# First-layer expert rows for 32 dense tokens from gathered rows, and VectorE's second-layer work in pairs of tiles

## The chip, the cores and the metric

The kernel runs on one NeuronCore of a Trainium2 chip. A core has TensorE (matmuls; its weight loads are listed as PEld beside PE), VectorE (DVE), ScalarE (ACT), GpSimd (POOL), the issuing queue SyncE (SP) and 16 DMA engines that all queues share. The metric is device time in microseconds (us) from launch to end, the median of several runs; lower is better.

## What is computed

The program is two transformer blocks on one sequence of 512 tokens of width 1024. The part that matters here is the last one, a PEER layer: 16,384 experts, each of them one row `u` and one row `v` of 1024 numbers. Each token picks 16 experts for each of 8 heads, so 128 picks:

```
q = (xb @ w_pq).reshape(PEER_BLOCK, PEER_HEADS, 2, D_KEY // 2)
s = einsum("thpd,hpnd->thpn", q, sub_keys)
s_top, i_top = lax.top_k(s, PEER_TOPK)
cand = s_top[:, :, 0, :, None] + s_top[:, :, 1, None, :]
best, ci = lax.top_k(cand, PEER_TOPK)
e = i1 * N_KEYS + i2
gate = softmax(best)
act = gelu(einsum("thkd,td->thk", u_exp[e], xb))
out = einsum("thk,thkd->td", gate * act, v_exp[e])
```

## The kernel before, in words

The PEER layer is done in two ways. For the first 128 tokens (one per partition) the picked rows are **gathered**: GpSimd issues an indirect DMA that brings 128 rows of 4 KB (one per token), VectorE multiplies the `u` rows with the tokens and sums them (`dot`, L1965, a custom instruction), and later adds the `v` rows times their coefficients to a sum in PSUM (`axpy`, L2097). 128 picks make 128 dots and 128 row sums. Seven row buffers (`GR`) rotate: a gather waits until the row seven places before it has been used.

For the other `TD` = 384 tokens the layer is **dense**, over all 16,384 experts in `NE` = 128 tiles of 128 experts. In the **first layer** (`up(e)`, L2795) TensorE multiplies a `u` tile with the 384 tokens: 8 chunks of the width times 3 products, since every 32-bit operand is split in a high and a low half (high times high, high times low, low times high). ScalarE makes the high half of a weight tile (`split_high`, L1368), GpSimd the low half (`split_low`, L867), into one of two buffers; `split_high(e + 2)` waits until `up(e)` has finished. ScalarE applies gelu (L1374) and SP stores the activations to DRAM (`expert_acts`). Meanwhile VectorE searches the picks (`for t in range(NT)`), and from tile `FIRST_SPREAD` = 52 on, for 48 tiles, the gates are spread: per tile VectorE builds one-hot matrices for 8 tokens (L2081, L2082, L2084), TensorE multiplies them (16 short matmuls, L2812), and ScalarE stores the product, a gate for each token and expert (0 where not picked), to `gates_spread` in DRAM.

In the **second layer** (`down(e, c)`, L2825) SP loads activations and gates back, VectorE multiplies them (`weigh`, L2107), ScalarE and VectorE split the product (`weighted_high`, L1402; `weighted_low`, L2113), and TensorE multiplies it with the `v` tile: 2 halves of the width times 3 groups of 128 tokens times 3 products, 18 matmuls of 512 columns per tile. The low half of even `v` tiles comes from GpSimd (L867), that of odd ones from VectorE (`odd_low`, L2120), in four buffers (`WS`).

The order on each engine is written out by hand. GpSimd issues gather j behind the `split_low` of the tile that `gather_after(j)` names. VectorE runs dots inside the search (`between`), after each one-hot batch (5 for 3 batches), and in the second layer `axpys_by(e)` row sums, 14 for 13 tiles, from tile 4 on.

## Time and profile before

| | |
|---|---|
| three runs | 2490.09, 2494.13, 2505.22 us, median 2494.13 |
| profiled execution, span | 2489.0 us |
| PE busy | 2441.9 us (98%) |
| DVE busy | 1589.9 us (64%) |
| POOL busy | 1304.9 us (52%) |
| ACT busy | 961.0 us (39%) |
| DMA | 508.91 MB, mean 204 GB/s |
| granted TensorE clock, mean | 0.997 of full speed |

The profiled execution's own time is not listed apart from these three; its span is 1.1 us below the fastest of them and 5.1 us below the median. Times in rows are microseconds from the start of the span, "mean ns" is one instruction. The time in brackets at the end of a row is how long the engine sat idle before it, and what ended that. The first layer of the experts runs from about 1321 to 1944 us, the second from 1944 to about 2471.

### The profile page before, as it was taken

What the parts mean: (1) busy time and instruction counts of PE and PEld (TensorE: products, weight loads), DVE (VectorE), ACT (ScalarE), POOL (GpSimd) and SP (SyncE); (2) the same over time, 40 slices, a digit from 0 to 9 for tenths busy, and PEclk for the clock granted to TensorE, in tenths of its full rate; (3) what the DMA queues carried; (4) which work ended last, traced back from release to release, by engine and by line L of the source; (5) the groups of instructions that cost most, each with busy time, mean ns of one, the idle gap of its engine ahead of it and who ended that gap; (6) DMA issues with size and microseconds to landing.
All of it is one profiled execution on the core that took longest, in us unless ns stands there. A gap on an engine that the chain in (4) does not pass through costs nothing.

```text
span 2489.0 us, 32824 instructions
## 1 busy us (share of the span) xinstructions
PE 2441.9 (98%) x12339; PEld 2069.7 (83%) x12339; DVE 1589.9 (64%) x2580; ACT 961.0 (39%) x1565; POOL 1304.9 (52%) x698
## 2 busy tenths in 40 slices
PE   9999999999999999999999999999999999999998
PEld 6877766778786777787789999999999888888886
DVE  3247255766403635332479897998940799999995
ACT  3256455222224445523333334343433433333333
POOL 3651423444454433144434887666666566676662
PEclk9999999999999999999999999999999999999999
DMA  5320112655433222032223888999997899999992
GB/s 215 119 85 1 60 60 95 199 196 177 153 102 118 85 78 76 26 102 91 95 85 125 297 304 283 359 354 361 359 320 258 304 363 360 364 368 362 363 364 88
DMA packets 212733, 508.91 MB, mean 204 GB/s; under 512 B 18400, under 2 KB 101344, under 8 KB 212192
## 3 DMA queue, kind: packets, MB, share of 16 engines
q1 hardware_dynamic: 123696, 338.22, 38.8%
q0 software_dynamic: 36864, 134.23, 15.1%
q10 hardware_dynamic: 52016, 34.36, 4.4%
q8 instruction: 99, 1.62, 0.3%
q14 instruction: 58, 0.48, 0.1%
HBM read 454.31 MB, written 52.43 MB: 204 GB/s over the span
## 4 chain that ended last, share of the span: by engine, by line
PE 89%; POOL 3%; DVE 3%; ACT 3%; issue 1%; DMA 1%; SPq 0%; ACTq 0%; DVEq 0%
PE bank L2211 73%; PE bank L2812 3%; PE bank_and L2211 3%; POOL weight_split L851 3%; PE bank L2346 3%; PE bank_and L2179 2%; PE bank L2336 1%; ACT weight_split L992 1%; DMA ring<-weights 1%; PE bank_and L2311 1%; PE bank L2311 1%; PE bank L2190 0%; PE bank_and L2625 0%; DVE h_split L1471 0%; POOL weight_split L867 0%
## 5 line engine op out<-in xcount | busy, mean ns | idle before, releaser
L2211 PE MATMUL bank<-h_split,weight_split 128*128 128x384 f32 (+1 forms) x5568 | 1135.3, 362 | 16.1 <-POOL weight_split L851 6.6
L2211 PEld LDWEIGHTS bank<-h_split,weight_split 128*128 128x128 f32 x5568 | 995.1, 188 | 130.5 <-POOL weight_split L851 16.4
L851 POOL TENSOR_TENSOR weight_split<-ring,weight_split 128x1024 fp32r<-128x1024 f32 x182 | 453.8, 2494 | 721.3 <-ACT weight_split L992 721.1
L2211 PE MATMUL bank<-late_weight_split,weighted_split 128*128 128x512 f32 x2268 | 515.1, 389 | 0.2 <-DVE weighted_split L2113 0.2
L2211 PEld LDWEIGHTS bank<-late_weight_split,weighted_split 128*128 128x128 f32 x2268 | 425.4, 188 | 88.9 <-issue 0.6
L878 POOL DMA_INDIRECT arena<-weights,arena x256 | 312.6, 1221 | 147.0 <-DVE arena L1965 60.0
L867 POOL TENSOR_TENSOR weight_split<-ring,weight_split 128x1024 fp32r<-128x1024 f32 x129 | 310.1, 2404 | 120.5 <-ACT weight_split L1368 119.5
L992 ACT ACTIVATE weight_split<-ring 128x1024 fp32r<-128x1024 f32 x182 | 191.9, 1054 | 293.4 <-PE bank L2211 273.8
L1368 ACT ACTIVATE weight_split<-ring 128x1024 fp32r<-128x1024 f32 x130 | 137.6, 1060 | 390.6 <-PE bank L2211 335.3
L2107 DVE TENSOR_TENSOR arena<-arena 128x384 f32<-128x384 f32 x128 | 227.0, 1773 | 20.3 <-DMA arena<-expert_acts 19.9
L867 POOL TENSOR_TENSOR late_weight_split<-ring,late_weight_split 128x1024 fp32r<-128x1024 f32 x63 | 151.9, 2411 | 103.7 <-ACT late_weight_split L1368 103.1
L1965 DVE CUSTOM_DVE_ANT_0 arena<-arena,bank_and 128x1024 f32<-128x1024 f32 x128 | 153.1, 1218 | 47.8 <-DMA arena<-weights,arena 46.8
L1402 ACT ACTIVATE weighted_split<-arena 128x384 fp32r<-128x384 f32 x128 | 67.3, 526 | 269.4 <-DVE arena L2107 258.8
L2097 DVE SCALAR_TENSOR_TENSOR bank_and<-arena,bank_and 128x1024 f32<-128x1024 f32 x127 | 162.6, 1281 | 0.9
L1368 ACT ACTIVATE late_weight_split<-ring 128x1024 fp32r<-128x1024 f32 x126 | 132.6, 1052 | 46.6 <-PE bank L2211 40.9
L2211 PE MATMUL bank<-hidden_layer_split,weight_split 128*128 128x512 f32 x528 | 122.3, 392 | 1.3 <-POOL weight_split L851 1.0
L2211 PEld LDWEIGHTS bank<-hidden_layer_split,weight_split 128*128 128x128 f32 x528 | 98.2, 188 | 25.0 <-issue 2.6
L1533 DVE SCALAR_TENSOR_TENSOR arena<-bank,rstd 128x512 f32<-128x512 f32 x42 | 29.0, 692 | 124.4 <-PE bank L2211 116.1
L2113 DVE TENSOR_TENSOR weighted_split<-arena,weighted_split 128x384 fp32r<-128x384 f32 x128 | 74.1, 579 | 47.3 <-ACT weighted_split L1402 47.3
L2812 PE MATMUL bank<-arena 128*128 128x128 f32 x768 | 93.4, 275 | 0.0
L2812 PEld LDWEIGHTS bank<-arena 128*128 128x128 f32 x768 | 92.3, 192 | 0.0
L2346 PEld LDWEIGHTS bank<-arena 128*128 128x128 f32 x528 | 67.4, 191 | 22.0 <-ACT arena L1027 13.4
(367 smaller groups left out, 2724.7 us busy)
## 6 DMA issues: line engine op xcount, KB each, us to landing
ring<-weights SPq DMA_DIRECT2D x493, 512.0 KB
expert_acts<-arena SPq DMA_DIRECT2D x128, 192.0 KB
gates_spread<-arena ACTq DMA_DIRECT2D x24, 1024.0 KB
arena<-gates_spread SPq DMA_DIRECT2D x96, 256.0 KB
arena<-expert_acts SPq DMA_DIRECT2D x128, 192.0 KB
arena<-weights,arena POOLq DMA_INDIRECT x256
arena<-bias_sel ACTq DMA_DIRECT2D x1, 2048.0 KB, 7.7
arena<-bias_band ACTq DMA_DIRECT2D x1, 2048.0 KB, 8.2
```

The lines of the kernel that those rows point to most:

```text
L851: nc.gpsimd.tensor_tensor(w_split[:, (count - 1) % 2, 1, :], ring[:, n % RING, :], w_split[:, (count - 1) % 2, 0, :], ALU.subtract).then_i ...
L867: nc.gpsimd.tensor_tensor(w[:, 1, :], ring[:, (BEFORE + e) % RING, :], w[:, 0, :], ALU.subtract).then_inc(w_lo_ready, 1)
L878: nc.gpsimd.indirect_dma_start(gathered_rows[:, j % GR, :], None, expert_rows, bass.IndirectOffsetOnAxis(ap=pick, axis=0)).then_inc(gather ...
L992: a.activation(w_split[:, s % 2, 0, :], ring[:, n % RING, :], ACT.Copy).then_inc(w_high, 1)
L1368: a.activation(split_of(e)[:, 0, :], ring[:, n % RING, :], ACT.Copy).then_inc(w_hi_ready, 1)
L1965: v.tensor_tensor_reduce(rows_, rows_, wide[:, :], 1.0, 0.0, ALU.mult, ALU.add, dots[:, j:j + 1]).then_inc(gather_used, 1)
L2097: v.scalar_tensor_tensor(out=wide[:, :], in0=rows_, scalar=coef[:, j:j + 1], in1=wide[:, :], op0=ALU.mult, op1=ALU.add).then_inc(gather_us ...
L2107: v.tensor_tensor(weighed[:, e % 2, :], act_in[:, e % AS, :], gblk[:, b % 2, :, j], ALU.mult).then_inc(weighed_ready, 1)
L2113: v.tensor_tensor(p_split[:, e % PS, 1, :], weighed[:, e % 2, :], p_split[:, e % PS, 0, :], ALU.subtract).then_inc(p_lo_ready, 1)
L2211: ins = mm(*args, start=start, stop=stop)
L2346: last = mm(bank[4 + g % 2][:, h * HD:(h + 1) * HD], probT[:, u % 2, c * P:(c + 1) * P], vals(i, c), start=(c == 0), stop=(c == blocks(i) ...
L2812: mm(bank[2 + n % 3][:, (t % 4) * P:(t % 4 + 1) * P], hot1[:, t % HOT, :], hot2[:, t % HOT, :], start=True, stop=True).then_inc(hot_used, 1)
```

## The change

Of the 384 dense tokens the first `XC` = 32 leave the dense first layer, so `up(e)` works on `TU` = 352 tokens and the stored activations are 352 wide. The 32 tokens have 32 x 128 = 4096 picks; laid out as 128 partitions by `CC` = 32 columns (four partitions for a token) they are 32 more gathers and dots, ahead of the 128 of the first kind. Their tokens are repeated four times by ScalarE (`few_wide`) and put into PSUM by 16 matmuls; row numbers go out to DRAM and back in the new layout, and so do the finished dots, after which ScalarE applies gelu and VectorE multiplies them into the gates before the gates are spread. In the second layer the activations of these 32 tokens are a constant 1.0 (one memset), so their products with the spread gates are already complete. The second layer of the 32 tokens stays dense.

The search takes the tokens in the order 1, 0, 2, 3; `FIRST_SPREAD` goes from 52 to 56; 3 dots for 2 batches run in place of 5 for 3. Of 160 dots 128 are done by the end of the first layer, the other 32 in the second, tiles 2 to 24; the 128 row sums follow from tile 26 to 120. Both come at 8 for 3 pairs of tiles. VectorE's second-layer loop is written per pair.

```diff
+XC = 32
+CC = PICKS * XC // P
+TU = TD - XC
+UP_ROWS = CC + PICKS
...
-        FIRST_SPREAD = 52
-        SPREAD_DOTS = TOP_DOTS + BATCHES * 5 // 3
-        AXPY_FROM = 4
+        FIRST_SPREAD = 56
+        SPREAD_DOTS = TOP_DOTS + BATCHES * 3 // 2
+        UP_DOTS = SPREAD_DOTS + 20
+        AXPY_FROM = 26
...
+        def dots_by(e):
+
+            return min(UP_DOTS + e // 2 * 8 // 3, UP_ROWS)
...
-            return min(max((e - AXPY_FROM + 1) * 14 // 13, 0), PICKS)
+            return min(max((e - AXPY_FROM) // 2 + 1, 0) * 8 // 3, PICKS)
...
             if j < GR:
-                return 13 + j * 2 // 3
+                return 15 + j * 2 // 3
             n = j - GR
             if n < TOP_DOTS:
-                return 17 + n
+                return 18 + n
...
+                if e == FEW_ROWS_AT:
+                    sp.wait_ge(rows_ready, 1)
+                    sp.dma_start(by_token[0], few_rows).then_inc(few_moved, 16)
+                elif e == FEW_ROWS_AT + 1:
+                    sp.wait_ge(few_moved, 16)
+                    sp.dma_start(few_row_at, turned_dram[0]).then_inc(few_moved, 16)
+                elif e == FEW_DOTS_AT:
+                    sp.wait_ge(gather_used, CC)
+                    sp.dma_start(turned_dram[1], few_dots).then_inc(few_moved, 16)
+                elif e == FEW_DOTS_AT + 1:
+                    sp.wait_ge(few_moved, 48)
+                    sp.dma_start(few_gelu, by_token[1]).then_inc(few_moved, 16)
...
-            for t in range(NT):
+            for t in SEARCH_ORDER:
...
+                if t == 1:
+                    dve.wait_ge(dots_gelu, 1)
+                    v.tensor_tensor(gates_[0:XC], gates_[0:XC], few_gelu, ALU.mult).then_inc(chosen_ready, 1)
...
-                dots_to(TOP_DOTS + (batch + 1) * 5 // 3)
-            dots_to(PICKS)
+                dots_to(TOP_DOTS + (batch + 1) * 3 // 2)
+            link(v.memset(act_in[:, :, 0:XC], 1.0))
+            dots_to(UP_DOTS)
...
             weigh(0)
+            weigh(1)
+            weighted_low(0)
+            odd_low(NE + 1)
+            weighted_low(1)
             summed = 0
-            for e in range(NE):
-                if e + 1 < NE:
-                    weigh(e + 1)
-                    if e == 0:
-                        weighted_low(e)
-                    if (e + 1) % 2:
-                        odd_low(NE + e + 1)
-                if e:
-                    weighted_low(e)
-                if e == AXPY_FROM - 1:
-                    dve.wait_ge(dots_gelu, 1)
+            for e in range(2, NE, 2):
+                dve.wait_ge(w_hi_ready, NE + e + 1)
+                if e == AXPY_FROM:
+                    dve.wait_ge(dots_gelu, 2)
                     link(v.tensor_tensor(coef, dots, gate0, ALU.mult))
+                dots_to(dots_by(e))
                 while summed < axpys_by(e):
                     axpy(summed)
                     summed += 1
+                weigh(e)
+                weigh(e + 1)
+                weighted_low(e)
+                weighted_low(e + 1)
+                odd_low(NE + e + 1)
...
-                    x = [h_split[:, part, k, P:T] for part in range(2)]
-                    last = products(bank[e % 2][:, 0:TD], w, x, k == 0, k == KD - 1)
+                    x = [h_split[:, part, k, P + XC:T] for part in range(2)]
+                    last = products(bank[e % 2][:, 0:TU], w, x, k == 0, k == KD - 1)
```

How the order moves on VectorE, in the middle of the second layer. L2097 before and L2158 now is the row sum, L2107 and L2168 `weigh`, L2120 and L2181 `odd_low`, L2113 and L2174 `weighted_low`; `weighted_split_61` holds the split product, `late_weight_split_62` the split weights. Before:

```order
L2097 SCALAR_TENSOR_TENSOR bank6_and_7<-arena,bank6_and_7 128x1024 [waits gathered_rows_used,rows_gathered4]
L2107 TENSOR_TENSOR arena<-arena 128x384 [waits p_lo_ready,act_loaded1]
L2120 TENSOR_TENSOR late_weight_split_62<-ring,late_weight_split_62 128x1024 [waits w_hi_ready]
L2113 TENSOR_TENSOR weighted_split_61<-arena,weighted_split_61 128x384 [waits p_hi_ready]
L2097 SCALAR_TENSOR_TENSOR bank6_and_7<-arena,bank6_and_7 128x1024 [waits gathered_rows_used,rows_gathered5]
L2107 TENSOR_TENSOR arena<-arena 128x384 [waits p_lo_ready,act_loaded2]
L2113 TENSOR_TENSOR weighted_split_61<-arena,weighted_split_61 128x384 [waits p_hi_ready]
```

and now:

```order
L2158 SCALAR_TENSOR_TENSOR bank6_and_7<-arena,bank6_and_7 128x1024 [waits gathered_rows_used,rows_gathered0,w_hi_ready]
L2158 SCALAR_TENSOR_TENSOR bank6_and_7<-arena,bank6_and_7 128x1024 [waits gathered_rows_used,rows_gathered1]
L2168 TENSOR_TENSOR arena<-arena 128x384 [waits p_lo_ready,act_loaded0,gates_loaded0]
L2168 TENSOR_TENSOR arena<-arena 128x384 [waits p_lo_ready,act_loaded1]
L2174 TENSOR_TENSOR weighted_split_61<-arena,weighted_split_61 128x384 [waits p_hi_ready] x2
L2181 TENSOR_TENSOR late_weight_split_62<-ring,late_weight_split_62 128x1024 [waits w_hi_ready]
```

The row sums (here two, in two pairs of three it is three) stand together at the head of a pair, behind a wait for the high half of the pair's even weight tile; the two `weigh`, the two `weighted_low` and the `odd_low` follow them.

On GpSimd, in the same stretch, `DMA` rows are gathers and `TENSOR_TENSOR` rows the low half of even tiles. Before:

```order
L878 DMA arena<-weights,arena 128x1024 [waits gathered_rows_used] x2
L867 TENSOR_TENSOR late_weight_split<-ring,late_weight_split 128x1024 [waits w_hi_ready]
L878 DMA arena<-weights,arena 128x1024 [waits gathered_rows_used] x3
L867 TENSOR_TENSOR late_weight_split<-ring,late_weight_split 128x1024 [waits w_hi_ready]
L878 DMA arena<-weights,arena 128x1024 [waits gathered_rows_used] x2
```

and now:

```order
L907 TENSOR_TENSOR late_weight_split<-ring,late_weight_split 128x1024 [waits w_hi_ready]
L921 DMA arena<-weights,arena 128x1024 [waits gathered_rows_used] x3
L907 TENSOR_TENSOR late_weight_split<-ring,late_weight_split 128x1024 [waits w_hi_ready]
L921 DMA arena<-weights,arena 128x1024 [waits gathered_rows_used] x2
L907 TENSOR_TENSOR late_weight_split<-ring,late_weight_split 128x1024 [waits w_hi_ready]
```

Behind each low half come two or three gathers, three in two cases of three; before it was two, and three once in every six or seven.

## Rows read from the trace of the kernel before

**Rows 1.** Windows: length, busy (instructions) per engine, clock, DMA share, GB/s.

```profile
1950.00:2430.00 480.00, 479.18 (x2113) 396.43 (x2114) 476.25 (x421) 180.37 (x237) 324.27 (x181) 1.00 0.99 363
1560.00:1824.00 264.00, 264.00 (x1777) 264.00 (x1776) 241.31 (x286) 107.38 (x179) 178.97 (x120) 1.00 1.03 358
```

**Rows 2.** Timeline of PE, last first-layer tiles: start, length, line, tiles, count.

```profile
1827.87 116.73 PE L2211 MATMUL bank<-h_split,weight_split 128*128 128x384 f32 x672
```

**Rows 3.** Timeline of PE, late in the second layer.

```profile
2399.79 63.64 PE L2211 MATMUL bank<-late_weight_split,weighted_split 128*128 128x512 f32 x280
```

**Rows 4.** Timeline, ScalarE and GpSimd in a plain first-layer tile.

```profile
1940.54 1.06 ACT L1368 ACTIVATE weight_split<-ring 128x1024 fp32r<-128x1024 f32 x1 [2.72 <-PE bank L2211]
...
1941.68 2.40 POOL L867 TENSOR_TENSOR weight_split<-ring,weight_split 128x1024 fp32r<-128x1024 f32 x1 [1.77 <-ACT weight_split L1368]
```

**Rows 5.** Timeline of three engines where PE did wait for GpSimd.

```profile
1547.42 4.12 PEld L2211 LDWEIGHTS bank<-h_split,weight_split 128*128 128x128 f32 x24
...
1551.82 2.37 POOL L867 TENSOR_TENSOR weight_split<-ring,weight_split 128x1024 fp32r<-128x1024 f32 x1
1551.95 1.06 ACT L1368 ACTIVATE weight_split<-ring 128x1024 fp32r<-128x1024 f32 x1 [3.54 <-PE bank L2211]
...
1554.30 1.86 PEld L2211 LDWEIGHTS bank<-h_split,weight_split 128*128 128x128 f32 x11 [0.86 <-ACT arena L1374]
```

**Rows 6.** Timeline of GpSimd at the first gathers.

```profile
1372.85 2.40 POOL L867 TENSOR_TENSOR weight_split<-ring,weight_split 128x1024 fp32r<-128x1024 f32 x1 [1.74 <-ACT weight_split L1368]
1375.41 1.15 POOL L878 DMA_INDIRECT arena<-weights,arena  x1 [0.17 <-issue]
...
1377.83 2.41 POOL L867 TENSOR_TENSOR weight_split<-ring,weight_split 128x1024 fp32r<-128x1024 f32 x1
```

**Rows 7.** Timeline, steady second layer: GpSimd, VectorE and ScalarE.

```profile
2197.42 2.40 POOL L867 TENSOR_TENSOR late_weight_split<-ring,late_weight_split 128x1024 fp32r<-128x1024 f32 x1
2197.62 2.95 DVE L2107 TENSOR_TENSOR arena<-arena 128x384 f32<-128x384 f32 x1
...
2201.03 1.04 ACT L1368 ACTIVATE late_weight_split<-ring 128x1024 fp32r<-128x1024 f32 x1
2202.15 0.88 DVE L2107 TENSOR_TENSOR arena<-arena 128x384 f32<-128x384 f32 x1
2202.50 1.35 POOL L878 DMA_INDIRECT arena<-weights,arena  x1 [1.10 <-DVE bank_and L2097]
2202.94 1.22 DVE L2120 TENSOR_TENSOR late_weight_split<-ring,late_weight_split 128x1024 fp32r<-128x1024 f32 x1
2203.06 0.53 ACT L1402 ACTIVATE weighted_split<-arena 128x384 fp32r<-128x384 f32 x1 [0.99 <-DVE arena L2107]
2204.08 0.55 DVE L2113 TENSOR_TENSOR weighted_split<-arena,weighted_split 128x384 fp32r<-128x384 f32 x1
```

**Rows 8.** Timeline of VectorE, two row sums back to back.

```profile
2433.03 2.67 DVE L2097 SCALAR_TENSOR_TENSOR bank_and<-arena,bank_and 128x1024 f32<-128x1024 f32 x2
```

**Rows 9.** The page, costliest groups: the dots on VectorE.

```profile
L1965 DVE CUSTOM_DVE_ANT_0 arena<-arena,bank_and 128x1024 f32<-128x1024 f32 x128 | 153.1, 1218 | 47.8 <-DMA arena<-weights,arena 46.8
```

**Rows 10.** The page, DMA issues: count and KB each.

```profile
ring<-weights SPq DMA_DIRECT2D x493, 512.0 KB
expert_acts<-arena SPq DMA_DIRECT2D x128, 192.0 KB
...
arena<-gates_spread SPq DMA_DIRECT2D x96, 256.0 KB
```

**Rows 11.** Windows of 8.16 us in the second layer.

```profile
2023.44:2031.60 8.16, 8.16 (x38) 6.76 (x37) 8.16 (x9) 3.06 (x4) 5.21 (x4) 1.00 1.03 402
2096.88:2105.04 8.16, 8.16 (x38) 6.76 (x37) 8.16 (x9) 3.06 (x4) 5.20 (x4) 1.00 0.92 284
```

**Rows 12.** Timeline at the change of layers: PE and VectorE.

```profile
1950.63 4.35 PE L2211 MATMUL bank<-weight_split,weighted_split 128*128 128x512 f32 x18 [1.91 <-DVE weighted_split L2113]
...
1952.07 0.90 DVE L2107 TENSOR_TENSOR arena<-arena 128x384 f32<-128x384 f32 x1 [1.58 <-DMA arena<-expert_acts]
```

More of the change, by code:

```diff
@@ L884, in _ @@
                     split_low(e)
-                while issued < 2 * PICKS and gather_after(issued) <= e:
+                while issued < UP_ROWS + PICKS and gather_after(issued) <= e:
                     gather(issued)
                     issued += 1
-            assert issued == 2 * PICKS
+            assert issued == UP_ROWS + PICKS
             for k in range(1, 4):
@@ L1975, in between @@
             def between(t):
-                if t and dotted[0] < TOP_DOTS // ND * t:
+                if dotted[0] < TOP_DOTS // ND * SEARCH_ORDER.index(t):
                     dots_to(dotted[0] + 1)
@@ L2816, in _ @@
                 up(e)
+                if e == 2:
+                    pe.wait_ge(few_spread, 2)
+                    pe.wait_ge(score_out, 16)
+                    for k in range(KD):
+                        for part in range(2):
+                            last = mm(few_x[:, k * P:(k + 1) * P], few_wide[:, part, k, :], ident, start=(part == 0),
+                                      stop=(part == 1))
+                    last.then_inc(x_rows, 1)
                 if e == FIRST_SPREAD - 1:
```

87 lines of the change are left out of this document (61 added, 26 removed).

## Prediction, made before the changed kernel was run

> **What bounds the kernel now.** I read the windows first. In the second layer [rows 1] PE is busy 479 of 480 us, VectorE 476, and the DMA share is 0.99 at 363 GB/s: three resources stand at their limit together. In the first layer with its one-hot batches PE is busy 264 of 264 us and DMA has a share of 1.03. The granted clock is 1.00 of 2.4 GHz in both. So PE sets the time of the whole stretch that the change touches, and the question is which of the others takes over where PE is relieved or they are loaded. The timelines give PE's pace: 672 matmuls of 384 columns in 116.73 us, 173.5 ns each [rows 2], 24 to a tile, so 4.163 us a tile; 280 of 512 columns in 63.64 us, 226.7 ns each [rows 3], 18 to a tile, 8.16 us for a pair. With a one-hot batch there are 40 matmuls per tile, 1777 in 264 us [rows 1], 5.94 us a tile; a batch of 16 costs 1.78.
>
> **First layer, the matmuls.** The two widths give the price of a column: (226.7 - 173.5) / 128 = 0.416 ns. Cutting 32 columns saves 13.3 ns each, 0.32 us a tile: 3.84 in place of 4.163. In the 48 tiles with a batch PE has only itself to wait for: 48 x 0.32 = 15.3 us.
>
> The other 80 tiles cannot take all of it. Split weights have two buffers, so tile e + 2 is bound to the end of tile e: from the first weight load of a tile to ScalarE's next high half 4.53 us (1547.42 to 1551.95) [rows 5], from there to GpSimd's start 1.14 and GpSimd 2.40 [rows 4], and 0.11 until PE loads (GpSimd ends at 1554.19, PE starts at 1554.30) [rows 5]. That is 8.18 for two tiles, against 8.33 that PE needs: now hidden by 0.15. With 352 columns the loop is 8.18 - 0.32 = 7.86, 3.93 a tile, and PE would need only 3.84. So the loop decides: 80 x (4.163 - 3.93) = 18.6 us. What was cover becomes the bound, and GpSimd's lateness costs directly from here on.
>
> **First layer, what is added.** 16 matmuls of 128 columns after tile 2: a batch, 1.8 us. Spreading the tokens is two ScalarE instructions of 1024 columns, 1.06 each by the high half [rows 4], in a tile with over 2 us of idle ScalarE: nothing. SP gets four small transfers with waits; the ring is four tiles ahead, so its cover is over 10 us, and it would cost only if the 32 dots were not done by tile 47: nothing. GpSimd's first gathers come two to a tile, and there its halves start 4.98 us apart [rows 6], 0.8 above PE's present need and 1.05 above 3.93. The change has such tiles at 15 and 17 and one of three gathers at 19. I count 3.2 us against 1.2 now: 2.0. The exponentials are issued two whole tiles ahead of the turn of the gates, a lead that shrinks by 2 x 0.23: 0.5 us if it had none to spare, and I charge that.
>
> **The change of layers.** PE waits 1.91 us for VectorE's low half of tile 1, which the new order makes earlier: gone. Late next is tile 2: its low half now stands behind the multiply of tile 3, whose activations land at 1952.07 [rows 12]; 0.90 and 0.55 more make 1953.5, where PE is due 4.08 after 1948.72, at 1952.8. 0.7 remains, 1.2 us are saved.
>
> Together 15.3 + 18.6 - 1.8 - 2.0 - 0.5 + 1.2 = 30.8 us saved before the second layer's pace is asked.
>
> **Second layer.** PE's work is unchanged, 8.16 a pair. Two things could become longer. First **VectorE**. Now one multiply of each pair starts beside GpSimd's subtraction and takes 2.95 us in place of 0.88, ending 0.75 after it [rows 7]. The row sums, which read PSUM, and the dots, 1218 ns on average [rows 9], show no such lengthening. The new order puts them beside the subtraction: two sums take 2.67 [rows 8], the subtraction 2.40 [rows 7], and both start on the same signal. The chain of a pair is then: 8/3 sums at 1.33, 3.55; multiply 0.88; ScalarE's copy, high half and copy, 0.53 + 1.04 + 0.53; VectorE's low half 0.55 and odd split 1.22 [rows 7, 8]. That is 8.27 with every end fully awaited; instructions that follow on one engine start some 0.09 before the last one ends (2202.15 + 0.88 against 2202.94) [rows 7], four times, so 7.9. PE has 8.16: no cost at 7.9, 7 us in 60 pairs at 8.27. I take 0. GpSimd has 2.40 and 8/3 gathers at 1.35 [rows 7], 6.0.
>
> Second **DMA**. A pair moved two weight tiles, two activation tiles, one and a half gate blocks [rows 10] and 28/13 gathers of 512 KB: 2.96 MB in 8.16 us, 363 GB/s, just what the window shows, so DMA moved what was asked. Now the activations fall to 176 KB and the gathers rise to 8/3: 3.20 MB, 392 GB/s. The ends: windows in the second layer reach 402 GB/s [rows 11], which would cost nothing; 363 as a ceiling would make a pair 8.82, 60 x 0.66 = 40 us more. The window with 284 GB/s at a share of 0.92 [rows 11] shows that the rate also falls without an idle queue. I take the upper end, less a little for such dips: 3 us. The nearest row is the one of 402, since it is the same mix at a demand above average.
>
> A rule speaks against that choice. The Trainium skill, "DMA: Bandwidth & Descriptors", section "Where 436 GB/s comes from", puts the limit of one core's HBM traffic at about 358 GB/s and the vendor's model at 368. At 358 a pair would take 8.94 us and the stretch 47 us more, an estimate by which the kernel would be some 16 us slower than before. The trace already holds 363 over 480 us and 402 for a while, so the first figure is not a ceiling here; the measurement decides, though nothing shows 392 for long.
>
> **Sum.** 30.8 - 3 = 28 us. Against the profiled span of 2489.0 that is 2461; the median of the runs lies 5.1 above the span, so 2466.
>
> **The rivals.**
> DMA becomes the bound in the second layer. For it: share 0.99 already, the dips, 19% more gathered bytes per pair. Against: 402. A ceiling of 380 makes a pair 8.42 and costs 16 us, a kernel of 2479; 363 gives 2503.
> The loop over two buffers is not there, PE keeps its 13.3 ns everywhere and GpSimd's lateness is absorbed: 128 x 0.32 = 40.8, less 1.8 and 0.5, plus 1.2, 39.7 saved: 2454. Against it stands the sum of rows 4 and 5.
> The chain of VectorE and ScalarE is 8.27 or a little more: 2473 to 2480.
> The matmuls do not get shorter, since the weight loads bind: PEld is busy 264.00 of 264 us in the first layer [rows 1], and the number of loads stays. Then 33.9 is lost and the kernel takes about 2500. The Trainium skill, "Perfetto Trace Analysis", section "Identifying the Most-Contended Engine", tells to judge TensorE by the busy share of LDWEIGHTS, and by that PE has no headroom here. Against it: 16 short matmuls take 1.78 us [rows 1, 2], 111 ns for a load and a product, so loads can follow each other far faster than every 173 ns.
> Slower: the multiplies still meet the subtraction. GpSimd's subtraction stands in line behind gathers, each of which waits for the row sum seven places before; if the last gather of a pair ends late, the subtraction starts late and holds both the multiply and the chain behind it, 2.95 - 0.88 = 2.07 us a pair. In all 60 pairs: 7.9 + 2.07 = 9.97 against 8.16, 109 us, a kernel of 2572. Below 0.26 us a pair it costs nothing, and it makes the kernel slower than before once it takes 0.77 a pair, some four pairs in ten. Against it: GpSimd has 2 us to spare in a pair, and its gathers can all be issued by about 7 us.
>
> **Chances.** Forecast 0.48 (2457 to 2474), DMA 0.23, no loop 0.08, the longer chain 0.08, loads bind 0.04, multiplies still held 0.09. The range takes the forecast, the fast rival, and DMA down to about 365 GB/s: 2452 to 2500. One per cent, 25 us, is about what can be told from no change here. Faster by more: the forecast below 2469, 0.40, and the fast rival, 0.08: 0.48. Slower by more: held multiplies and a worse DMA, 0.11. Between: 0.41.
>
> **What would show it.** In the profile after: first-layer matmuls 160 ns apart in tiles with a batch and tiles of 3.93 without, with short waits of PE for GpSimd's half in the latter; if the tiles are 3.84, the loop was wrong; if 4.16, the columns. In the second layer PE pairs of 8.16, multiplies of 0.88 and none of 2.95, DMA near 390 GB/s. PE waiting there for VectorE's low half, while VectorE waits for activations or gathered rows, means that DMA bounds. What would make the forecast wrong first is the rate that DMA can hold, then any regular lateness of GpSimd.

## The result and the profile after

The changed kernel takes **2466.9 us** (median of 17 runs, 2463.33 to 2494.76), the kernel before 2491.63 (17 runs, 2489.45 to 2505.22). The ratio is 0.9903, 95% interval 0.9885 to 0.9921: 24.7 us less. The forecast was 2466 in a range of 2452 to 2500. That the number agrees does not make the terms right. The profiled execution has a span of 2469.1 us (2470.95 with what lies around it); against the profiled 2489.0 of before it saves 19.9 where the prediction's sum said 28.

The same windows as in [rows 1], a little shorter in the second layer because the kernel ends earlier:

```profile
1950.00:2400.00 450.00, 449.75 (x1985) 372.19 (x1984) 397.35 (x452) 161.35 (x224) 335.56 (x202) 1.00 1.03 399
1560.00:1824.00 264.00, 262.57 (x1818) 262.41 (x1818) 239.67 (x280) 108.79 (x184) 175.43 (x116) 1.00 1.03 348
```

PE is still full in both. VectorE, to which work was added, shows less busy time (88% against 99%), and DMA moves 399 GB/s where it moved 363. PE in the first layer (start, length, line, tiles, count, wait ahead), which answers to [rows 2]:

```profile
1331.20 3.73 PE L2886 MATMUL bank_and<-const,arena 128*128 128x128 f32 x32
...
1386.93 7.84 PE L2275 MATMUL bank<-h_split,weight_split 128*128 128x352 f32 x48 [0.55 <-POOL weight_split L907]
1395.23 7.85 PE L2275 MATMUL bank<-h_split,weight_split 128*128 128x352 f32 x48 [0.46 <-POOL weight_split L907]
1404.78 142.19 PE L2275 MATMUL bank<-h_split,weight_split 128*128 128x352 f32 x864 [1.69 <-POOL weight_split L907]
...
1554.93 4.05 PE L2275 MATMUL bank<-h_split,weight_split 128*128 128x352 f32 x24
...
1562.19 4.05 PE L2275 MATMUL bank<-h_split,weight_split 128*128 128x352 f32 x24 [1.43 <-POOL weight_split L907]
...
1567.78 4.24 PE L2275 MATMUL bank<-h_split,weight_split 128*128 128x352 f32 x24
1571.85 1.95 PE L2876 MATMUL bank_and<-arena 128*128 128x128 f32 x16
1573.56 4.24 PE L2275 MATMUL bank<-h_split,weight_split 128*128 128x352 f32 x24
```

There are two tile lengths beside the one-hot batches: 4.05 to 4.07 for the first three tiles and 4.24 for the other 45, at a granted clock of 1.00. The first matmul of such a row takes 0.24 to the second and the last 0.33; the 22 steps between are 158 ns in the short row and 167 in the long one. A tile with its batch takes 5.78 (1567.78 to 1573.56); it was 5.94, and 5.62 was forecast. In the plain tiles 864 matmuls, 36 tiles, run in 142.19 us: 3.950 a tile, forecast 3.93. The starts of the single matmuls show that this is a mean of two things: 25 of the 35 tiles between the first start and the last one have the pitch of 158 ns and take 3.92, with a stall of 0.1 to 0.2 us at the end of nearly every second one, and 10 have 166 to 167 ns and take 4.02. The matmuls of `few_x` are 32 in the profile and take 3.5 us.

The first layer begins at 1319.46 (before 1321.21, in code that was not touched), its batches at 1549.32 and the second layer at 1924.15. With the same places of before, against the sum on record:

| part, profiled spans | before | after | saved | forecast |
|---|---|---|---|---|
| up to the first layer | 1321.21 | 1319.46 | 1.75 | 0 |
| 80 plain tiles with `few_x` and waits | 334.55 | 323.81 | 10.7 | 18.6 - 1.8 - 2.0 = 14.8 |
| turn of the gates | 2.26 | 2.32 | -0.1 | -0.5 |
| 48 tiles with a batch | 286.42 | 278.56 | 7.9 | 15.3 |
| second layer to the end | 544.56 | 544.95 | -0.4 | 1.2 - 3 = -1.8 |
| sum | 2489.0 | 2469.1 | 19.9 | 27.8 |

PE's waits for others around the first layer (total us, times, longest), which hold what [rows 5] and [rows 12] were about:

```profile
PE bank L2275 <- POOL weight_split L907: 6.0, 6, 1.7
PE bank_and L2275 <- DVE weighted_split L2174: 2.3, 3, 1.4
PE bank L2275 <- DVE arena L2130: 1.1, 1, 1.1
```

VectorE's multiplies `weigh` and GpSimd's low halves in 1960 to 2400, before and after (count, busy us, mean ns of one, idle time before them):

```profile
L2107 DVE TENSOR_TENSOR arena<-arena 128x384 f32<-128x384 f32 x109 | 197.0, 1807 | 0.0
```

```profile
L2168 DVE TENSOR_TENSOR arena<-arena 128x384 f32<-128x384 f32 x108 | 92.9, 900 | 3.9 <-DMA arena<-expert_acts 3.9
```

```profile
L907 POOL TENSOR_TENSOR late_weight_split<-ring,late_weight_split 128x1024 fp32r<-128x1024 f32 x55 | 153.2, 2786 | 74.7 <-ACT late_weight_split L1411 74.7
```

So the multiplies of 2.95 us of [rows 7] are gone, as forecast; GpSimd's low half, 2.40 in [rows 7], is now 2.79 on average. It now starts while `odd_low` is still running, and is longer by about the time that the two overlap:

```profile
2161.51 1.22 DVE L2181 TENSOR_TENSOR late_weight_split<-ring,late_weight_split 128x1024 fp32r<-128x1024 f32 x1
2162.03 2.96 POOL L907 TENSOR_TENSOR late_weight_split<-ring,late_weight_split 128x1024 fp32r<-128x1024 f32 x1 [1.32 <-ACT late_weight_split L1411]
```

Of the 55 low halves in 1960 to 2400, those that overlap `odd_low` by 0.7 us take 2.94 to 2.97, and the ten that overlap it by 0.1 or less take 2.40 or 2.41; `odd_low` itself stays at 1.22. The row sums beside them make no difference to either.

### The profile page after: what moved, and what is told of

Read it like the earlier page. It is cut to its first block, busy times and chain, and to the rows that moved or that the text cites. A ratio compares the mean times of both kernels' runs of the same rounds, so it can differ in the third digit from the quotient of the medians.

```text
span 2469.1 us, 33014 instructions
## 1 busy us (share of the span) xinstructions
PE 2420.5 (98%) x12371; PEld 2040.6 (83%) x12371; DVE 1532.1 (62%) x2649; ACT 951.0 (39%) x1568; POOL 1332.3 (54%) x730
## 4 chain that ended last, share of the span: by engine, by line
PE 87%; POOL 4%; DVE 3%; ACT 3%; DMA 2%; issue 1%; SPq 0%; ACTq 0%; DVEq 0%
PE bank L2275 60%; PE bank_and L2275 14%; PE bank L2410 3%; POOL weight_split L891 2%; PE bank_and L2876 2%; PE bank_and L2243 2%; PE bank_and L2400 1%; PE bank L2876 1%; DMA ring<-weights 1%; ACT weight_split L1035 1%; POOL weight_split L907 1%; DMA arena<-expert_acts 1%; PE bank_and L2375 1%; PE bank L2375 1%; PE bank L2748 0%
## 5 line engine op out<-in xcount | busy, mean ns | idle before, releaser
L2275 PE MATMUL bank<-h_split,weight_split 128*128 128x352 f32 (+1 forms) x5472 | 1086.1, 356 | 17.2 <-POOL weight_split L907 6.0
L2275 PEld LDWEIGHTS bank<-h_split,weight_split 128*128 128x128 f32 x5472 | 943.9, 188 | 133.6 <-issue 15.2
L2275 PE MATMUL bank<-late_weight_split,weighted_split 128*128 128x512 f32 x1512 | 363.8, 390 | 0.0
L2275 PEld LDWEIGHTS bank<-late_weight_split,weighted_split 128*128 128x128 f32 x1512 | 283.7, 188 | 58.8
L907 POOL TENSOR_TENSOR late_weight_split<-ring,late_weight_split 128x1024 fp32r<-128x1024 f32 x63 | 175.7, 2789 | 106.4 <-ACT late_weight_split L1411 106.4
L2018 DVE CUSTOM_DVE_ANT_0 arena<-arena,bank_and 128x1024 f32<-128x1024 f32 x160 | 191.2, 1217 | 62.4 <-DMA arena<-weights,arena 60.9
L2275 PE MATMUL bank_and<-late_weight_split,weighted_split 128*128 128x512 f32 x756 | 192.2, 390 | 2.3 <-DVE weighted_split L2174 2.3
L2158 DVE SCALAR_TENSOR_TENSOR bank_and<-arena,bank_and 128x1024 f32<-128x1024 f32 x127 | 163.4, 1286 | 12.1 <-ACT late_weight_split L1411 3.4
L2275 PEld LDWEIGHTS bank_and<-late_weight_split,weighted_split 128*128 128x128 f32 x756 | 141.7, 188 | 32.8 <-issue 3.5
L2168 DVE TENSOR_TENSOR arena<-arena 128x384 f32<-128x384 f32 x128 | 117.9, 960 | 13.2 <-DMA arena<-expert_acts 10.4
L2174 DVE TENSOR_TENSOR weighted_split<-arena,weighted_split 128x384 fp32r<-128x384 f32 x128 | 72.8, 569 | 66.0 <-ACT weighted_split L1445 65.0
L2275 PE MATMUL bank_and<-h_split,weight_split 128*128 128x512 f32 x384 | 91.8, 396 | 0.3 <-POOL weight_split L891 0.3
```

Of the source, the lines that this page charges most:

```text
L907: nc.gpsimd.tensor_tensor(w[:, 1, :], ring[:, (BEFORE + e) % RING, :], w[:, 0, :], ALU.subtract).then_inc(w_lo_ready, 1)
L2018: v.tensor_tensor_reduce(rows_, rows_, x[:, :], 1.0, 0.0, ALU.mult, ALU.add, n).then_inc(gather_used, 1)
L2158: v.scalar_tensor_tensor(out=wide[:, :], in0=rows_, scalar=coef[:, j:j + 1], in1=wide[:, :], op0=ALU.mult, op1=ALU.add).then_inc(gather_us ...
L2168: v.tensor_tensor(weighed[:, e % 2, :], act_in[:, e % AS, :], gblk[:, b % 2, :, j], ALU.mult).then_inc(weighed_ready, 1)
L2174: v.tensor_tensor(p_split[:, e % PS, 1, :], weighed[:, e % 2, :], p_split[:, e % PS, 0, :], ALU.subtract).then_inc(p_lo_ready, 1)
L2275: ins = mm(*args, start=start, stop=stop)
```

## The experiments

Four questions were open: whether the added work costs anything beside the narrower matmul; what the pairs are worth; why a tile with a batch takes 5.78 and not 5.62; and how near the second layer stands to DMA's limit. Twelve runs follow, two of them of the changed kernel itself. Each is compared with the kernel before on its own chip; where only parts are compared, the places are the same as in the table above.

### The changed kernel again

> The changed kernel once more, beside the other kernels of this group on one chip. Expected: 2467 us, within 2.

2473.3 us, median of 4 runs (2465.05 to 2475.93), ratio 0.9899 (0.9851 to 0.9946). Run again with the last three kernels:

> The changed kernel once more, as the one that the next three are held against on the same chip. Expected: 2467 to 2473 us, the values that it had before.

2465.3 us, 6 runs (2463.92 to 2474.6), ratio 0.9883 (0.9857 to 0.9909). The profiled spans were 2473.3 and 2472.8. PE's waits for GpSimd differed, 5.4 and 7.0 us in 8, and the first layer began at 1319.64 and 1321.43. The first lies outside the 2 us that were expected. So the kernel scatters by some 10 us, and single profiles must be compared part by part.

### The narrower matmul alone

```diff
 # the kernel before
+XC = 32
-    x = [h_split[:, part, k, P:T] for part in range(2)]
-    last = products(bank[e % 2][:, 0:TD], w, x, ...)
+    x = [h_split[:, part, k, P + XC:T] for part in range(2)]
+    last = products(bank[e % 2][:, 0:TD - XC], w, x, ...)
```

> The kernel before, with its first expert layer on 352 columns in place of 384 and nothing else; the first layer of 32 tokens of the dense block is left out and a constant stands in its place (no gathered rows, no added dots, no few_x matmuls, no pairs). Theory: the whole gain is the narrower matmul, and what the change adds beside it costs 1.8 (few_x) and about 2 (waits for the first gathers) on TensorE. Then this kernel is at 2467 less 4, 2463. Within it, a plain tile is 3.95 us or a little less, and a tile beside a gate batch goes from 5.94 to 5.78 if the 166.7 ns pitch of 352 columns belongs to the width and to a fully fed TensorE, to 5.56 if that pitch came from something that the change added (the dots, the gathers). Rival: the 166.7 ns pitch is the added work's doing; then 48 x 0.22 = 10.6 more is saved, and the time is 2452.

2468.7 us, 10 runs (2458.4 to 2485.53), ratio 0.9896 (0.9867 to 0.9925). Its profile gives 320.66 us for the plain tiles, 276.38 for the batches and 545.04 for the rest, from the start of the first layer 1144.3 in place of 1149.6: 5.3 us below the changed kernel. The time is 4.6 us below the changed kernel run beside it, and the ranges overlap. So the narrower matmul brings all the gain, and the added work costs a few us (4 was expected): 3.2 in the plain tiles. The 2.2 in the batches are in part the pitch, as follows. Of the 48 tiles beside a batch, 26 took 4.24 or 4.26 and 22 took 4.04 or 4.05, without dots or gathers of the change:

```profile
1690.76 4.24 PE L2214 MATMUL bank<-h_split,weight_split 128*128 128x352 f32 x24
1694.84 1.05 PE L2815 MATMUL bank<-arena 128*128 128x128 f32 x8
1696.51 1.16 PE L2815 MATMUL bank<-arena 128*128 128x128 f32 x8 [0.62 <-ACT arena L1385]
1697.43 4.05 PE L2214 MATMUL bank<-h_split,weight_split 128*128 128x352 f32 x24
1701.32 1.95 PE L2815 MATMUL bank<-arena 128*128 128x128 f32 x16
```

The slow pitch belongs to this width, and here it ended behind a wait of 0.62 us. A wait does not always end it: in the first run of the changed kernel again a tile behind a wait of 1.42 is slow,

```profile
1564.47 4.24 PE L2275 MATMUL bank<-h_split,weight_split 128*128 128x352 f32 x24 [1.42 <-POOL weight_split L907]
```

where the same tile behind 1.43 took 4.05 above. The theory's 5.78 a tile is there, and beside it 5.59 (1552.23 to 1557.82), near the rival's 5.56.

### Pairs alone, and the change without pairs

```diff
 # the kernel before; only VectorE's order
-            for e in range(NE):
-                if e + 1 < NE:
-                    weigh(e + 1)
...
+            for e in range(2, NE, 2):
+                dve.wait_ge(w_hi_ready, NE + e + 1)
...
+                weigh(e)
+                weigh(e + 1)
+                weighted_low(e)
+                weighted_low(e + 1)
+                odd_low(NE + e + 1)
```

> The kernel before with VectorE's second-layer work in pairs of tiles, and nothing else: all 384 dense columns stay on TensorE. Theory: TensorE sets the second layer at 4.08 us a tile with and without pairs, so 2491 us, within 2; the multiplies of the weights by the gates fall from 1.77 us to about 0.96 us each, because in a pair they stand clear of GpSimd's subtraction, and VectorE's busy time falls by about 100 us, none of it on the path. Rival: VectorE was late at some tiles of the second layer and pairs alone take 5 to 10 us off: 2482 to 2486. Third: work in pairs hands the first tile of a pair over later, and TensorE waits: above 2495.

2489.4 us, 10 runs (2487.71 to 2504.66), ratio 0.9975 (0.995 to 1.0): no change that can be told, as the theory had it. The multiplies fell to 0.91 us (0.96 was expected) and VectorE's busy time in 1950 to 2400 by 80 us, from 446 to 366 (100 was expected). The reverse experiment takes the changed kernel and undoes the pairs:

```diff
 # the changed kernel; only VectorE's order and its rates
-            for e in range(2, NE, 2):
+            for e in range(NE):
+                if e + 1 < NE:
+                    weigh(e + 1)
...
-    return min(UP_DOTS + e // 2 * 8 // 3, UP_ROWS)
+    return min(UP_DOTS + max(e - 1, 0) * 4 // 3, UP_ROWS)
```

> The changed kernel with VectorE's second-layer work back in single tiles, the dots and row sums of the gathered rows spread at the same mean rate (4/3 a tile). Theory: the pairs are what makes room for the added dots. The multiplies go back from 0.96 to 1.77 us each, 128 x 0.81 = 104 us, which on top of VectorE's 397 of 450 us makes 501: a tile takes at least 4.5 us in place of 4.08 and the kernel about 2467 + 51 = 2518, range 2500 to 2530. Rival: the longer multiplies hold time in which VectorE has nothing to do (they wait for GpSimd's subtraction and something else waits less), and the time stays within 5 of 2467.

2469.5 us, 4 runs (2462.1 to 2476.88), ratio 0.9887 (0.9835 to 0.9938). The theory said 2518 and is wrong; the rival holds. Its windows and multiplies in the second layer:

```profile
1950.00:2400.00 450.00, 450.00 (x1987) 372.63 (x1986) 446.37 (x454) 166.96 (x223) 351.19 (x205) 1.00 1.02 395
```

```profile
L2168 DVE TENSOR_TENSOR arena<-arena 128x384 f32<-128x384 f32 x109 | 157.1, 1442 | 0.0
```

The kernel before in the same window:

```profile
1950.00:2400.00 450.00, 449.18 (x1980) 371.60 (x1981) 446.25 (x395) 169.01 (x222) 307.16 (x172) 1.00 0.99 364
```

VectorE does 454 instructions in the same 446 us of busy time in which it did 395. That is 32 more rows used, since a dot has two records, the second of 0.08 us. The room came from the multiplies themselves: 1807 ns on average before, 1442 here, 900 in pairs; 109 multiplies became 40 us shorter in all, and 32 rows at 1.22 to 1.28 us are 40 us. In the 1807 there is a time in which the multiply stands held beside GpSimd's subtraction [rows 7], and it is booked as busy. **Busy time of that kind is slack.** VectorE's 99% was not a bound.

### The pitch of a matmul and its width

The kernel before on 368 and on 320 columns, one run each, edited like the one on 352 (`XC = 16`, `XC = 64`).

> The kernel before with its first expert layer on 368 columns (the first layer of 16 tokens is left out). It asks what a matmul's pitch is as its width goes. At 384 columns it was 173.3 ns in every tile, at 512 226.7 ns, both 32 cycles over the width. Theory: two pitches, one of 32 cycles over the width when weight loads fit, one of 400 cycles (166.7 ns) that is the width's or the weight load's floor in a fully fed TensorE. Then 368 columns take 400 cycles in every tile, batch or plain: 24 x 166.7 ns = 4.00 us, and a tile beside a gate batch takes the same 5.78 us as with 352 columns. Rival: the pitch is a fixed surplus of 28 or 48 cycles, then 165.0 or 173.3 ns.

> The kernel before with its first expert layer on 320 columns (the first layer of 64 tokens is left out). Theory: beside the gate batches a fully fed TensorE has a floor of 400 cycles (166.7 ns) a matmul, set by its weight loads; 320 columns then gain nothing over 352 there: 5.78 us a tile. In plain tiles the loop over the split buffers holds 3.9 us or a little less. Rival: the pitch goes on falling with the width, to 352 or 368 cycles (146.7 or 153.3 ns), and the batch tiles take 5.3 to 5.46 us; then the kernel is about 48 x 0.4 = 19 us faster than with 352 columns, as far as the GpSimd loop lets it.

Tiles beside a batch, of 368 columns, a row of plain ones of 368, and tiles of 320 beside a batch and in the plain part:

```profile
1691.67 4.24 PE L2214 MATMUL bank<-h_split,weight_split 128*128 128x368 f32 x24
...
1398.82 52.36 PE L2214 MATMUL bank<-h_split,weight_split 128*128 128x368 f32 x312
```

```profile
1692.83 3.76 PE L2214 MATMUL bank<-h_split,weight_split 128*128 128x320 f32 x24
...
1406.46 7.39 PE L2214 MATMUL bank<-h_split,weight_split 128*128 128x320 f32 x48 [0.17 <-POOL weight_split L869]
1414.01 7.39 PE L2214 MATMUL bank<-h_split,weight_split 128*128 128x320 f32 x48 [0.16 <-POOL weight_split L869]
```

At 368 columns a tile takes 4.24 beside a batch and 4.03 in the plain part (52.36 us for 13), 167 ns apart in both: the same as the slow pitch of 352. The expectation for 368 held, the one of a floor did not: at 320 columns all 48 tiles beside batches took 3.75 to 3.79 us, 147 ns apart, as its rival said. With 384 columns at 173.5 and 512 at 226.7 [rows 2, 3], four widths lie on one line of (columns + 32) / 2.4 ns. Only 352 is off it, at 158 or 167 and never the 160 of the line. So **beside the batches 352 columns cost what 368 cost** (batches 278.6 us in the changed kernel and 279.2 here), and the second half of the columns that the change removes pays only in the plain tiles. The times were 2473.3 and 2440.6 us, one run each, beside 2489.4 for before.

The 320 rows show the loop over the two split buffers as well: it takes 7.55 us for two plain tiles (1406.46 to 1414.01), with a wait for GpSimd in each of these rounds. The prediction's loop of 8.18 less 64 columns is 7.54, where PE alone would need 7.04. Where the profile lists no wait, as in a row of 336 matmuls in 52.86 us, two tiles still take 7.55: the stalls are below what it lists.

### A small matmul ahead of each tile

```diff
                 pe.wait_ge(w_lo_ready, e + 1)
+                if FIRST_SPREAD < e <= FIRST_SPREAD + BATCHES:
+                    mm(bank[e % 2][:, 0:8], w_split[:, e % 2, 0, 0:P], h_split[:, 0, 0, P + XC:P + XC + 8], start=True, stop=True)
                 for k in range(KD):
```

> The changed kernel with one matmul of 8 columns ahead of each first-layer tile that follows a one-hot batch (its result is overwritten). In the changed kernel a 352-column matmul took 166.7 ns in those tiles and 158.3 ns after TensorE had waited. Theory: the two pitches are two phases between the weight loads and the matmuls, which a wait resets and a short matmul may reset too. If it does, a tile beside a batch saves 24 x 8.3 ns = 0.20 us and pays 0.07 to 0.11 for the small matmul: 5.67 in place of 5.78, 5 us over 48 tiles. Rival: only an empty TensorE queue changes the phase; then the tile takes 5.88, and the kernel is 5 us slower.

```profile
1701.46 0.25 PE L2864 MATMUL bank<-h_split,weight_split 128*128 128x8 f32 x1
1701.57 4.06 PE L2275 MATMUL bank<-h_split,weight_split 128*128 128x352 f32 x24
1705.47 1.05 PE L2878 MATMUL bank_and<-arena 128*128 128x128 f32 x8
```

The theory holds in the profile. Every tile beside a batch is 4.04 to 4.08 us now. The tile with its batch takes 5.71, the small matmul 0.11 of it, and the batches 275.2 us in place of 278.6. Nothing of it reached the time: 2471.0 us, 6 runs (2469.62 to 2474.98), ratio 0.9910 (0.9883 to 0.9937), against 2465.3 for the changed kernel beside it, so if anything it is slower. In its profile the span was 4.2 us shorter than there, 2468.6 against 2472.8. 3.3 us are within the scatter; that it helps is not shown.

### GpSimd's part halved

```diff
-                w = split_of(e)
-                nc.gpsimd.tensor_tensor(w[:, 1, :], ring[...], w[:, 0, :], ...)
+                w, cols = split_of(e), slice(0, D // 2 if e < NE else D)
+                nc.gpsimd.tensor_tensor(w[:, 1, cols], ring[..., cols], w[:, 0, cols], ...)
```

> The changed kernel, with GpSimd's low half of the first-layer weights computed over 512 of 1024 columns (the low part of the other columns is left out; it keeps old values). Theory: in the plain tiles of the first layer the loop over two split buffers sets 3.95 us a tile. With GpSimd's part about halved the loop no longer binds, and a plain tile goes to 24 x 158.3 ns = 3.80 us, or, if a TensorE that never waits takes the 166.7 ns pitch at this width, to 4.00 us: then the shorter work makes the plain tiles slower by 0.05 us each. Whole time: 80 x 0.15 = 12 less (2455), or 80 x 0.05 = 4 more (2471). Rival: TensorE's own rate sets 3.95 and GpSimd is not in it: no change in the plain tiles.

One run: 2484.7 us, beside 2489.4 of before. Its first layer began at 1336.1, some 16 us late, with a granted clock of 0.89 in 200 to 400 us (0.98 in the changed kernel); that is not the edit's doing, and the parts behind it must speak. Two rows of plain tiles without any wait inside:

```profile
1480.66 38.24 PE L2275 MATMUL bank<-h_split,weight_split 128*128 128x352 f32 x240 [1.05 <-POOL weight_split L907]
...
1841.53 96.23 PE L2275 MATMUL bank<-h_split,weight_split 128*128 128x352 f32 x576
```

240 matmuls in 38.24 us are 3.80 a tile after the first, 576 in 96.23 are 4.00. Both branches of the expectation came true in one execution: freed of the loop, PE takes the fast pitch in these 10 tiles and the slow one in the 24 behind the batches. What chooses is not shown: behind this run's longest wait, 2.93 us ahead of 1426.77, the second to the seventh tile have 167 ns too. So the loop did hold the fast tiles of the changed kernel, at 3.92 in place of 3.80, and it costs little, since without it PE may be slower than with it. The plain tiles came to 321.7 us against 323.8; 5.0 of it were three waits, where ScalarE and with it GpSimd stood for a late weight transfer.

### One gather a tile at the start

```diff
-            if j < GR:
-                return 15 + j * 2 // 3
             n = j - GR
             if n < TOP_DOTS:
-                return 18 + n
+                return 14 + j
```

> The changed kernel, with its first gathers begun earlier and one a tile (they were two and three a tile on GpSimd, after which TensorE waited 2.7 us for the low half of the weights, in 3 waits). Theory: those waits go, and nothing else changes: 2.7 us less, within the scatter of the runs. Rival: the waits stand where the transfers of the weights and the gathers share the queues, and move to other tiles: no change.

2471.6 us, 6 runs (2464.93 to 2476.44), ratio 0.9905 (0.9877 to 0.9934): no gain. GpSimd and PE at the place:

```profile
1381.95 1.16 POOL L919 DMA_INDIRECT arena<-weights,arena  x1 [2.56 <-DMA arena<-picks_of_few_tokens]
1383.14 2.36 POOL L905 TENSOR_TENSOR weight_split<-ring,weight_split 128x1024 fp32r<-128x1024 f32 x1
```

```profile
1385.64 164.18 PE L2273 MATMUL bank<-h_split,weight_split 128*128 128x352 f32 x984 [2.07 <-POOL weight_split L905]
```

The waits for doubled gathers are gone, but the first gather is now due before its row numbers are back from DRAM, GpSimd stands 2.56 us, and PE waits 2.07 at once. Behind that wait the granted clock falls:

```profile
1385.64:1388.00 2.36, 2.35 (x12) 2.36 (x13) 0.44 (x1) 0.00 (x0) 2.32 (x2) 0.81 0.91 248
1388.00:1391.20 3.20, 3.20 (x15) 3.20 (x14) 2.21 (x10) 0.00 (x0) 1.98 (x2) 0.61 0.75 260
```

The first of the 41 tiles takes 5.53 us, with matmuls up to 294 ns apart, which is 352 columns at the lower level of 1.2 GHz; the other 40 take 3.97 each, near the 3.95 of the changed kernel. There the wait of 1.69 at the same place left the clock at 1.00. So one wait of 2.07, with some 1.7 us lost at the low clock behind it, took the place of three waits of 2.7 in all. Neither expectation named this. The two edits together:

> The small matmul and the single gathers together. If both theories hold, 7 to 8 us under the changed kernel, 2460 to 2465. If neither does, 5 us over it.

2468.4 us, 6 runs (2468.11 to 2487.39), ratio 0.9913 (0.9879 to 0.9948). The 2460 to 2465 did not come. None of these three kernels is told apart from the changed one as faster.

### More gathers in the second layer

```diff
-        UP_DOTS = SPREAD_DOTS + 20
-        AXPY_FROM = 26
+        UP_DOTS = SPREAD_DOTS
+        AXPY_FROM = 38
-            return min(UP_DOTS + e // 2 * 8 // 3, UP_ROWS)
+            return min(UP_DOTS + e // 2 * 3, UP_ROWS)
```

> The changed kernel with 3 gathered rows a pair of tiles all through the second layer in place of 8/3, the dots' gathers begun later, so that the second layer moves about 12% more gathered bytes. In the changed kernel DMA stood at 399 GB/s and a busy share of 1.03 there. Theory: the queues are not yet the bound, and TensorE keeps 8.16 us a pair: 2467, within 3, at about 410 GB/s. Rival: 399 GB/s is the ceiling, and the second layer stretches by about 3%, 13 us: 2480. A second rival: VectorE, 88% busy, is at 93% and its waits reach TensorE: 2470 to 2475.

One run: 2489.4 us. The second layer took 562.6 us, 17.6 more. The window, PE from one pair to the next, VectorE over the same pair, and all that VectorE waited for in 2150 to 2400 (total us, times, longest):

```profile
2150.00:2420.00 270.00, 269.62 (x1155) 213.93 (x1154) 242.01 (x257) 90.85 (x128) 212.56 (x129) 1.00 1.03 402
```

```profile
2156.65 1.61 PE L2275 MATMUL bank_and<-late_weight_split,weighted_split 128*128 128x512 f32 x6
...
2165.09 1.16 PE L2275 MATMUL bank_and<-late_weight_split,weighted_split 128*128 128x512 f32 x4
```

```profile
2157.65 1.22 DVE L2181 TENSOR_TENSOR late_weight_split<-ring,late_weight_split 128x1024 fp32r<-128x1024 f32 x1
2158.79 4.07 DVE L2158 SCALAR_TENSOR_TENSOR bank_and<-arena,bank_and 128x1024 f32<-128x1024 f32 x3
2162.76 1.71 DVE L2168 TENSOR_TENSOR arena<-arena 128x384 f32<-128x384 f32 x2
2164.38 0.56 DVE L2174 TENSOR_TENSOR weighted_split<-arena,weighted_split 128x384 fp32r<-128x384 f32 x1
2165.61 0.56 DVE L2174 TENSOR_TENSOR weighted_split<-arena,weighted_split 128x384 fp32r<-128x384 f32 x1 [0.66 <-ACT weighted_split L1445]
2166.08 1.22 DVE L2181 TENSOR_TENSOR late_weight_split<-ring,late_weight_split 128x1024 fp32r<-128x1024 f32 x1
```

```profile
DVE weighted_split L2174 <- ACT weighted_split L1445: 19.3, 29, 0.7
```

A pair takes 8.44 on PE (2156.65 to 2165.09) in place of 8.16, and 8.43 on VectorE (2157.65 to 2166.08). VectorE goes from one instruction to the next and waits only for ScalarE's second copy, which is part of the chain that the prediction added up; nobody waits for a transfer in this stretch. By the sizes in [rows 10], 3 gathers and not 8/3 make 3.38 MB a pair: 414 GB/s at 8.16, 400 at 8.44. So the 402 of the window is what the slower pairs asked for, and not a ceiling. The changed kernel holds the same chain: a pair with three row sums takes 8.44 there too, one with two 7.04.

```profile
2161.51 1.22 DVE L2181 TENSOR_TENSOR late_weight_split<-ring,late_weight_split 128x1024 fp32r<-128x1024 f32 x1
2162.64 4.07 DVE L2158 SCALAR_TENSOR_TENSOR bank_and<-arena,bank_and 128x1024 f32<-128x1024 f32 x3
...
2169.95 1.22 DVE L2181 TENSOR_TENSOR late_weight_split<-ring,late_weight_split 128x1024 fp32r<-128x1024 f32 x1
...
2176.99 1.22 DVE L2181 TENSOR_TENSOR late_weight_split<-ring,late_weight_split 128x1024 fp32r<-128x1024 f32 x1
```

Three pairs of it come to 7.97 on average, under PE's 8.16. With three sums in every pair nothing is given back: from 2090 on, 41 pairs in a row take 8.41 to 8.45. So the second rival has the mechanism, **the chain of VectorE and ScalarE reaches PE**, though it put the cost too low.

The 17.6 us add up from the starts of PE's matmuls. From 2136 on each pair has 0.27 more, 9.6 in all. Behind PE's two longest waits, 1.98 and 2.16, the granted clock was 0.57 in 1946 to 1950 and 0.59 in 2089 to 2093.2, which costs 3.2. The rest, 4.8, is mostly the waits themselves, of which 6.1 us are listed where the changed kernel has 2.3.

Only the pairs with dots, up to 2070, say something of DMA. There a pair with three dots takes 7.88 where nothing is late, but VectorE's multiplies waited for activations in most pairs, and 405 GB/s in 1962.64 to 2070.47 stood against the 414 asked. PE lost 0.4 us in that stretch. Whether this is the rate that DMA can hold, or these transfers were asked for too late, stays open. No run added bytes without adding work to VectorE.

## Why the prediction was right, and where it was not

- **What bounds.** PE did, as forecast, and still does. VectorE was named as a third resource at its limit. It was not: the single-tile order took in 32 more rows in 450 us at no cost. DMA was the second: it was not at its limit at 363 GB/s either, since it now moves 399.
- **First layer, the matmuls, 48 tiles with a batch: 15.3 forecast, 7.9 found.** This is the term that was most mis-sized. The price of a column was drawn from 384 and 512 columns, and 352 does not lie on that line. 45 tiles at 167 ns in place of the forecast 160 are 24 x 6.5 ns x 45 = 7.0 us, and one wait for GpSimd of 1.43 in place of 0.70 makes the rest. That the fast pitch would have paid the forecast is shown by the small matmul: 5.71 less its own 0.11 is 5.60, forecast 5.62.
- **The 80 plain tiles: 18.6 forecast, 17.8 found.** Without `few_x` and the listed waits a tile went from 4.176 to 3.954 us. The loop over the two split buffers is real and has the forecast size: 3.92 for the tiles of the fast pitch (forecast 3.93), 7.55 for two at 320 columns (7.54), and 3.80 in a row without it. The rival without a loop falls, and for a second reason, which nobody had in view: tiles at the slow pitch need 4.00 by themselves, and they are what lifts the mean over 3.93.
- **First layer, what is added.** `few_x` was put at 1.8 and took 3.5. It is 16 matmuls in the program and 32 in the profile, unlike the one-hot ones from which the price came; the same form stood ahead of the first layer in the kernel before. GpSimd's lateness was put at 2.0 and was 3.6: waits of 4.0 us in the plain tiles (0.55, 0.46, 1.69 and 1.34) against 0.4. The first three are at the doubled gathers that were named; the fourth, after the batches, was not foreseen. The exponentials cost 0.1 at most where 0.5 was charged.
- **The change of layers: 1.2 saved forecast, nothing found.** Tile 2 was late as said, for activations that land late, by 1.35 us and not 0.7, and tiles 4 and 6 by 0.72 and 0.25 more. Ahead of these three VectorE stood 2.10, 1.41 and 1.24 us for the activations of the pair's second tile. Whether the dots, which the sum left out here, made these transfers late was not tried. PE waits 2.3 us in all, before 2.1.
- **Second layer.** PE kept 8.16 a pair. The chain of VectorE and ScalarE fits on average, 7.97 with row sums against the forecast 7.9, and VectorE idles 53 of 450 us. But it fits only as a mean: 8.44 in two pairs of three. (Its terms add up to 8.30 and not 8.27; nothing hangs on that.) The row sums do not stand beside the subtraction from its start, as the prediction had it: `odd_low` does, and the subtraction takes 2.96 for it. The 3 us for dips did not come. For DMA the choice of the window with 402 as the upper end was right; the ceilings of 380 and 363 fall, and so does the 358 and 368 of the Trainium skill, "DMA: Bandwidth & Descriptors", section "Where 436 GB/s comes from", for this mix of transfers: 399 GB/s over 450 us. Where the rate ends was not found; 405 was held for 108 us.
- **Weight loads bind.** PEld is busy as long as PE again (262.41 of 262.57), and tiles still became shorter, so the busy share of LDWEIGHTS gave no bound, against the Trainium skill, "Perfetto Trace Analysis", section "Identifying the Most-Contended Engine". In one point the rival was nearer than the forecast knew: half of the removed columns brought nothing beside the batches.
- **Multiplies still held.** Not seen; 0.90 us on average.

So the median agrees better than the terms do, and that part is luck: the forecast took 28 us off a median of three runs, 2494.13, and over 17 runs that median is 2491.63. In the profiled executions 19.9 us were saved of 27.8, and 1.75 of these by chance ahead of the first layer; in the medians 24.7. The profiled executions of the changed kernel took 2 to 9 us more than the medians beside them, that of before 0.8 less than its median. Why stays open.

## What to carry to other kernels

Before an engine at 99% is called a bound, look at whether its long instructions are long because they are held: their mean falls as soon as real work comes. A price per column holds only at widths that were measured; look at the tile's length at the new width before more work is built around the columns it removes. Count the longest step of a chain and not only the mean: pairs of 8.44 cost nothing as long as every third one took 7.04, and one third of a row more per pair cost all that the change had won. And before a rate is called a ceiling, ask what was asked for: 402 GB/s was the demand of a stage that VectorE had slowed.

## What the runs showed of the hardware that was not expected

- A back-to-back matmul with its own weight load took (columns + 32) / 2.4 ns at 320, 368, 384 and 512 columns, and one of two values at 352: 158 or 167 ns at the same granted clock of 1.00. With one short matmul ahead of the tiles all 48 beside batches had the fast one, where the changed kernel had 3; behind a wait it was now the fast one (1.43 us) and now the slow one (1.42). A row once begun in either can keep it for ten tiles and more (576 matmuls at 167, 240 at 158). The cause between weight load and matmul was not isolated.
- DMA moved 399 GB/s for 450 us on one core, and 405 for 108 us, at a busy share of 1.03. At the first layer's mix the same share of 1.03 stood beside 348: the share tells that the engines are occupied, not the rate.
- A `weigh` or `odd_low` of VectorE and a subtraction of GpSimd do not run side by side: the one that started second was held. The multiply that started 0.20 us into the subtraction took 2.95 in place of 0.88 and left it at 2.40 [rows 7]; the subtraction that started 0.52 us into `odd_low` took 2.96 and left that at 1.22.
- Behind a wait of PE of about 2 us the granted clock fell in some places to the lower level, 1.2 GHz, and came back. From the first expert layer on, over all the profiles here, it fell behind 1.86, 1.88, 1.92, 1.98, 2.04, 2.07, 2.16 and 2.93 us and stayed behind 1.90, 1.91, 2.00 and 2.21, and behind all shorter ones. Each fall costs some 1.6 us more than the wait: 18 matmuls of the second layer took 5.97 us in place of 4.35 (the run on 368 columns at 1931.93, the kernel before at 1950.63).
